# Adaptive modulations of a three-layer network: one pass before the first projection, eight passes as 1 MB steps between tiles of three projections

## The reference, cut to what matters

```python
def adaln(cv, w, b):
    m = jax.nn.silu(cv) @ w + b
    m = m.reshape(cv.shape[:-1] + (1, N_MOD, D_MODEL))
    return [m[..., k, :] for k in range(N_MOD)]
...
        a_lat = rms_norm(h_lat, g_norm_mix[i]) * (1 + sc1) + sh1
...
        h_lat = h_lat + ga1 * o_lat
        f_lat = rms_norm(h_lat, g_norm_ffn[i]) * (1 + sc2) + sh2
        h_lat = h_lat + ga2 * conv_ffn(f_lat, w_ffn_up[i], w_ffn_conv[i], b_ffn_conv[i], w_ffn_down[i])
```

## Time and profile before

| | us |
|---|---|
| median of 3 runs | 4006.7 |
| lowest, highest | 4005.63, 4010.36 |
| the profiled execution's own time | 4006.12 |
| its span, first to last instruction | 4004.3 |
| PE busy / DVE / ACT / POOL in the span | 3547.1 / 1225.7 / 778.0 / 276.0 |
| mean granted TensorE clock | 0.933 |

### The profile page before, as it was taken

One profiled execution on the slowest core, in us unless ns is written; L12 is line 12 of the kernel. 1 busy time (PEld: TensorE's weight loads), 2 busy tenths in 40 slices (PEclk: granted clock), 3 DMA queues, 4 the chain that ended last, 5 costly groups with the idle time before them and its releaser, 6 DMA issues. The chain is left out here.

```text
span 4004.3 us, 65004 instructions
## 1 busy us (share of the span) xinstructions
PE 3547.1 (89%) x26956; PEld 2168.2 (54%) x26956; DVE 1225.7 (31%) x2683; ACT 778.0 (19%) x1448; POOL 276.0 (7%) x435
## 2 busy tenths in 40 slices
PE   3699999999999999999989659996997699999984
PEld 1155755555555566444435349993573455665544
DVE  0012322222200243222017574433323433333323
ACT  0012212111100133211010243322411122222210
POOL 2000000000000000000010000000000033333320
PEclk7799999999999999999989769997998699999996
DMA  9910101111111100222221000001102289999995
GB/s 382 428 54 28 54 27 53 53 53 47 45 57 41 58 27 27 79 74 69 72 80 52 7 1 4 4 4 40 58 23 79 100 301 356 359 354 362 353 364 210
DMA packets 88964, 484.26 MB, mean 121 GB/s; under 512 B 16706, under 2 KB 20834, under 8 KB 57392
## 3 DMA queue, kind: packets, MB, share of 16 engines
q1 hardware_dynamic: 72080, 442.35, 29.7%
q0 software_dynamic: 16672, 38.77, 3.0%
HBM read 466.11 MB, written 31.46 MB: 124 GB/s over the span
## 5 line engine op out<-in xcount | busy, mean ns | idle before, releaser
L534 PE MATMUL psum<-arena 128*128 128x512 f32 x1408 | 665.3, 594 | 4.2 <-ACT arena L372 4.2
L434 PE MATMUL psum<-arena 128*128 128x512 f32 x1328 | 634.4, 601 | 34.3 <-PEq L1138 17.0
L434 PEld LDWEIGHTS psum<-arena 128*128 128x128 f32 x1328 | 254.4, 192 | 223.4 <-issue 203.9
L534 PEld LDWEIGHTS psum<-arena 128*128 128x128 f32 x1408 | 266.7, 190 | 194.4 <-issue 173.2
L2888 PE MATMUL psum<-arena 128*64 128x256 f32 x3072 | 352.7, 378 | 14.5 <-DMA arena<-exp_w_in 14.1
L2888 PEld LDWEIGHTS psum<-arena 128*64 128x64 f32 x3072 | 231.3, 134 | 161.3 <-issue 54.3
L562 DVE SCALAR_TENSOR_TENSOR arena<-psum,arena 128x511 f32<-128x511 f32 (+1 forms) x132 | 83.2, 658 | 554.1 <-ACT arena L546 554.1
L536 PEld LDWEIGHTS psum<-arena 128*128 128x128 f32 x704 | 133.4, 190 | 170.5 <-issue 170.5
L536 PE MATMUL psum<-arena 128*128 128x256 f32 x704 | 210.1, 379 | 0.0
L436 PEld LDWEIGHTS psum<-arena 128*128 128x128 f32 x640 | 121.8, 190 | 156.2 <-issue 156.2
L546 ACT ACTIVATE arena<-psum,arena 128x768 f32<-128x768 f32 (+1 forms) x88 | 77.9, 885 | 644.0 <-PE psum L536 390.2
(11 more groups left out here) (487 smaller groups left out, 4769.9 us busy)
## 6 DMA issues: line engine op xcount, KB each, us to landing
arena<-exp_w_in SPq DMA_DIRECT2D x207, 1024.0 KB, 11.2
arena<-w_mod_r_in SPq DMA_DIRECT2D x18, 4096.0 KB, 23.9
arena<-w_ffn_up_in SPq DMA_DIRECT2D x88, 512.0 KB, 3.5
arena<-w_ffn_down_in SPq DMA_DIRECT2D x16, 1408.0 KB, 5.9
arena<-w_in_in SPq DMA_DIRECT2D x35, 512.0 KB, 3.5
arena<-yrows SPq DMA_DIRECT2D x4, 4096.0 KB, 12.7
arena<-w_even_in_in SPq DMA_DIRECT2D x17, 512.0 KB, 3.6
arena<-w_qkv_in SPq DMA_DIRECT2D x12, 512.0 KB, 3.5
```

The costliest lines, as they stand in the source:

```text
L434: mm = pe.matmul(ps[:, 2 * b, :], lhsT, src[:, k, 0:LAT], start=(k == 0), stop=(k == kt - 1))
L534: mm = pe.matmul(ps[:, 2 * b, :], lhsT, A[:, k, 0:LAT], start=(k == 0), stop=(k == KD - 1))
```

## The change

`modulations` becomes `first_modulations` with pass 0 alone: eight DMAs of 1 MB (128 partitions of 8 KB out of rows of 32 KB) into eight slots, eight steps of four calls, one `turn`. X is now the first DMA on POOL's queue. The sum of squares moves from POOL to ACT (squares) and DVE (sums), behind the wait for all six DMAs. Three weight tiles of `even_in` are begun instead of five.

The other eight passes are 64 steps of a class `Mods`, each a load of 1 MB on SP and four calls on PE. `even_in` does passes 1 and 2, one step after each of tiles 0 to 15, with one slot (its feed has three slots instead of five); both `ffn_up` do three passes each, a step after each of tiles 2 to 25, with two slots. ACT's copy, PE's `turn` and DVE's additions stand one, two and three tiles after the last step of a pass; those of pass 2 stand at the end of `even_in`. PSUM banks 6 and 7 hold the passes' sums, so the projections' tiles go round three pairs of banks instead of four, and `EV_JOBS` has u and r tiles between the vt jobs.

The layout of the matrices in HBM is unchanged. The core of the diff:

```diff
-        evi = Feed(nc, "evi", io["w_even_in"], KD)
-        modulations(nc, m, io, evi)
+        evi = Feed(nc, "evi", io["w_even_in"], KD, 3)
+        first_modulations(nc, m, io, evi)
...
-        even_in(nc, m, io, evi, Norm(m, T, 0, (0, 0)), tables)
+        even_in(nc, m, io, evi, Norm(m, T, 0, (0, 0)), tables, Mods(m, io, [1, 2], [OFF["W"] + 3 * KD * P], [6, 7]))
...
-        ffn_up(nc, m, 0, T, up, Norm(m, T, 1, (0, 3)), down)
+        spare = [BIG + (KF + 4) * T + u * MOD_PASS for u in range(2)]
+        ffn_up(nc, m, 0, T, up, Norm(m, T, 1, (0, 3)), down, Mods(m, io, [3, 4, 5], spare, [6, 7]))
...
-        ffn_up(nc, m, 1, LAT, up, Norm(m, LAT, 3, (1, 3)), down)
+        ffn_up(nc, m, 1, LAT, up, Norm(m, LAT, 3, (1, 3)), down, Mods(m, io, [6, 7, 8], spare, [6, 7]))
...
+class Mods:
...
+    def load(self, e, s, i):
+        n, k = self.passes[i // KD], i % KD
+        if i >= self.R:
+            e.wait_ge(s["mdm"], i - self.R + 1)
+        e.dma_start(self.m["at"](self.slots[i % self.R], MOD_PASS),
+                    self.w[(2 * n + k // 4) * P:(2 * n + k // 4 + 1) * P, k % 4 * MOD_PASS:(k % 4 + 1) * MOD_PASS]
+                    ).then_inc(s[f"mdw{i % self.R}"], 16)
+    def step(self, pe, s, i):
+        u, k = i // KD, i % KD
+        b = self.bank(u)
+        pe.wait_ge(s[f"mdw{i % self.R}"], 16 * (i // self.R + 1))
+        if k == 0 and u >= len(self.banks):
+            pe.wait_ge(s["mde"], 2 * (u - len(self.banks) + 1))
+        silu_c = self.m["at"](OFF["silu"], 2, KD, 32)[:, self.passes[u] // (2 * MOD_PASSES), k, :]
+        w = self.m["at"](self.slots[i % self.R], 4, 512)
+        for j in range(4):
+            mm = pe.matmul(self.m["ps"][32 * j:32 * j + 32, b, :], silu_c, w[:, j, :], start=(k == 0), stop=(k == KD - 1))
+        mm.then_inc(s["mdm"], 1)
...
+    def rows(self, act, s, u):
+        act.wait_ge(s["mdm"], KD * (u + 1))
+        if u:
+            act.wait_ge(s["mdt"], u)
+        act.activation(self.rows_at, self.m["ps"][:, self.bank(u), :], ACT.Copy).then_inc(s["mdr"], 1)
...
+    def turn(self, pe, s, u):
+        pe.wait_ge(s["mdr"], u + 1)
+        for c in range(4):
+            t = pe.matmul(self.m["ps"][:, self.bank(u), 8 * c:8 * c + 8], self.rows_at[:, c * P:(c + 1) * P], self.pick,
+                          start=True, stop=True)
+        t.then_inc(s["mdt"], 1)
...
+    def between(self, e, s, first, w):
+        i = w - first + self.R - 1
+        if self.R <= i < self.N:
+            self.load(e, s, i)
+    def begin(self, e, s):
+        for i in range(min(self.R, self.N)):
+            self.load(e, s, i)
...
+def first_modulations(nc, m, io, then):
+    mods = Mods(m, io, [0], [BIG + u * MOD_PASS for u in range(KD)], [0])
...
-            for n in range(CH):
-                u = n % NS
-                if n >= NS:
-                    sp.wait_ge(s["mm"], n - NS + 1)
-                sp.dma_start(slots[:, u, :, :].rearrange("p k n -> p (k n)"),
-                             io["w_mod_r"][n * P:(n + 1) * P, :]).then_inc(s[f"w{u}"], 16)
+            mods.begin(sp, s)
...
+            pool.dma_start(X, io["xT"].rearrange("(k p) n -> p k n", p=P)).then_inc(s["x"], 16)
             for name in ("ident", "ones", "bones", "rw_masks", "rst64"):
                 pool.dma_start(m[name], io[name]).then_inc(s["x"], 16)
-            pool.dma_start(m["X"], io["xT"].rearrange("(k p) n -> p k n", p=P)).then_inc(s["x"], 16)
...
-            ss, sq, X = m["at"](NRM_SS, T), m["at"](NRM_SQ, 2, T), m["X"]
-            pool.tensor_tensor(ss, X[:, 0, :], X[:, 0, :], MUL).then_inc(s["ss"], 1)
-            for k in range(1, KD):
-                if k >= 3:
-                    pool.wait_ge(s["ss"], k - 1)
-                pool.tensor_tensor(sq[:, k % 2, :], X[:, k, :], X[:, k, :], MUL).then_inc(s["sq"], 1)
-                pool.wait_ge(s["sq"], k)
-                pool.wait_ge(s["ss"], k)
-                pool.tensor_tensor(ss, ss, sq[:, k % 2, :], ADD).then_inc(s["ss"], 1)
...
-            for n in range(NP):
...
+            act.wait_ge(s["x"], 16 * 6)
+            for k in range(KD):
+                if k >= 3:
+                    act.wait_ge(s["ss"], k - 2)
+                act.activation(ss if k == 0 else sq[:, k % 2, :], X[:, k, :], ACT.Square).then_inc(s["sq"], 1)
+            mods.rows(act, s, 0)
...
+            for i in range(KD):
+                mods.step(pe, s, i)
+            pe.wait_ge(s["x"], 16 * 6)
+            mods.turn(pe, s, 0)
...
+            for k in range(1, KD):
+                dve.wait_ge(s["sq"], k + 1)
+                if k >= 2:
+                    dve.wait_ge(s["ss"], k - 1)
+                dve.tensor_tensor(ss, ss, sq[:, k % 2, :], ADD).then_inc(s["ss"], 1)
...
+    def __init__(self, nc, name, w, kt, slots=None):
         self.w, self.kt, self.n = w, kt, w.shape[0]
-        self.slots = 2 * KF // kt
+        self.slots = slots or 2 * KF // kt
...
+        for w in range(1, self.n):
+            t = w + self.slots - 1
+            if t < self.n or between is not None:
+                e.wait_ge(mm, w)
+            if t < self.n:
+                self.load(m, e, t)
+            if between is not None:
+                between(w)
...
-            feed.rest(m, sp, s["mm"])
+            mods.begin(sp, s)
+            feed.rest(m, sp, s["mm"], lambda w: mods.between(sp, s, 2, w))
...
-                b = t % 4
+                b = t % 3
                 feed.arrived(pe, t)
-                if t >= 4:
-                    pe.wait_ge(s["tp"], t - 3)
-                if t == 3:
+                if t >= 3:
+                    pe.wait_ge(s["tp"], t - 2)
+                if t == 2:
                     pe.wait_ge(s["nxn"], KD)
...
                 mm.then_inc(s["mm"], 1)
+                u, k = (t - 2) // KD, (t - 2) % KD
+                if 0 <= t - 2 < mods.N:
+                    mods.step(pe, s, t - 2)
+                if u and k == 1 and u <= len(mods.passes):
+                    mods.turn(pe, s, u - 1)
...
+                u, k = (t - 2) // KD, (t - 2) % KD
+                if u and k == 0 and u <= len(mods.passes):
+                    mods.rows(act, s, u - 1)
...
+                u, k = (t - 2) // KD, (t - 2) % KD
+                if u and k == 2 and u <= len(mods.passes):
+                    mods.add(dve, s, u - 1)
...
 EV_JOBS = [("z", 0), ("q", 0), ("q", 1), ("k", 0), ("k", 1), ("v", 0), ("g", 0), ("v", 1), ("g", 1), ("v", 2), ("g", 2), ("v", 3),
-           ("g", 3), ("u", 0), ("vt", 0), ("u", 1), ("vt", 1), ("u", 2), ("vt", 2), ("u", 3), ("vt", 3),
-           ("r", 0), ("r", 1), ("r", 2), ("r", 3)]
+           ("g", 3), ("u", 0), ("u", 1), ("vt", 0), ("u", 2), ("vt", 1), ("u", 3), ("vt", 2), ("r", 0), ("vt", 3),
+           ("r", 1), ("r", 2), ("r", 3)]
...
-    wg = at(OFF["W"] + feed.slots * KD * P, 2, 256)
+    wg = at(EV_WG, 2, 256)
...
-            feed.rest(m, sp, s["mm"])
+            mods.begin(sp, s)
+            feed.rest(m, sp, s["mm"], lambda w: mods.between(sp, s, 0, w))
...
-                sp.wait_ge(s["mm"], feed.last_over(lo, lo + n))
+                if lo < feed.slots * KD * P:
+                    sp.wait_ge(s["mm"], feed.last_over(lo, lo + n))
                 if lo + n > feed.slots * KD * P:
+                    sp.wait_ge(s["mdm"], mods.N)
+                if lo + n > EV_WG - OFF["W"]:
                     sp.wait_ge(s["gp"], 4)
...
-                b = j % 4
-                if j >= 4:
-                    pe.wait_ge(s[released[EV_JOBS[j - 4]][0]], released[EV_JOBS[j - 4]][1])
+                b = j % 3
+                if j >= 3:
+                    pe.wait_ge(s[released[EV_JOBS[j - 3]][0]], released[EV_JOBS[j - 3]][1])
...
+                if t == 0:
+                    pe.wait_ge(s["nxn"], KD)
+                if t < mods.N:
+                    mods.step(pe, s, t)
+                if t == KD + 1:
+                    mods.turn(pe, s, 0)
+            mods.turn(pe, s, 1)
...
+                if tiles[kind, i] in (KD, 2 * KD):
+                    mods.rows(act, s, tiles[kind, i] // KD - 1)
...
+            mods.add(dve, s, 0)
...
+            mods.add(dve, s, 1)
```

More of the change, by code:

```diff
@@ L175, with __init__, bank, add @@
 MOD_PASSES = MT * P // MOD_PASS
[L178 to L190 removed]
+class Mods:
+    def __init__(self, m, io, passes, slots, banks):
+        self.m, self.passes, self.slots, self.banks = m, passes, slots, banks
+        self.w = io["w_mod_r"]
+        self.R, self.N = len(slots), KD * len(passes)
+        self.SEMS = " mdm mdr mdt mde mdg " + " ".join(f"mdw{u}" for u in range(self.R)) + " "
+        self.rows_at = m["at"](OFF["rows"], 512)
+        self.pick = m["ident"].rearrange("p (j c) -> p j c", j=4)[:, :, 0:2]
+    def bank(self, u):
+        return self.banks[u % len(self.banks)]
+    def load(self, e, s, i):
[27 more added lines that the diff above has]
+        t.then_inc(s["mdt"], 1)
+    def add(self, dve, s, u):
+        m, n = self.m, self.passes[u]
+        l, t = n // MOD_PASSES, n % MOD_PASSES
```

(34 more changed lines are left out.)

76 lines of the change are left out of this document (12 added, 64 removed).

## The result

| | before | after |
|---|---|---|
| median, us | 4007.73 (4 runs) | 3919.85 (4 runs) |
| lowest, highest | 4005.63, 4010.36 | 3918.07, 3922.76 |
| span of the profiled execution | 4004.3 | 3916.3 |
| mean granted TensorE clock | 0.933 | 0.946 |

The ratio is 0.9781, with an interval of 0.9764 to 0.9798: 88 us faster, where 70 were forecast. Nine later runs of before and five of the changed kernel gave 4007.16 and 3922.19, ratio 0.9786 (0.9773 to 0.9799).

What follows compares the result with a forecast made beforehand. The first stage was taken as bound by its DMA loads, the projections by PE. From 4006.1 us, 158 saved in front and 88 added by steps and turns gave 3936, range 3914 to 3966.

Steps and rivals of the forecast that it cites:

- rival 5: Cheap seams and a fast front: 0.95 us a step, X at 36, time 3915; chance 0.07.
- When X is there: Front: X with the tables arrives at 38 us, between 36 and 41, reckoned from the bytes and queue rates.
- rival 2: Front: X comes as late as before, the front ends at 64, time 3951; chance 0.08.
- Squares and sums: Front, after X: two squares on ACT, then seven sums on DVE with handing over, 9.1 us in all.
- The tail: Front, after the sums: bank copy and `turn` run beside the last sum; DVE's bias and gains add 0.5 us.
- A step: Projections: four calls cost 1.25 us, 0.86 of it streaming and 0.39 array-shape changes; 64 steps are 80 us.
- Turn: Projections: `turn` after a pass's last step adds 1.0 us of weight loads; seven stand between tiles, 7 us.
- Its end in `even_in`: The eighth `turn`, of pass 2, with its copy and additions at the end of `even_in`: 0.8 us.
- What was put at nothing: Projections: loads, SP's waits, three pairs of banks, ACT's copies and DVE's additions are all covered, costing nothing.
- The 1 us of lost clock at `even_in`'s start: Norm's first PE calls run at half clock from the start, behind a front that is mostly waiting: 1 us more.
- signs named ahead: Marks of being right: `even_in`'s start, DMA share in front, gapless PE, tile distances, clock of 1.00, longer stage spans.
- Rivals 1 to 4: Dear seams, 3964, chance 0.10; late X, 3951, 0.08; slow strided loads, 3960, 0.05; steps lowering the clock, 4042, 0.04.

Runs made afterwards that it cites:

- e1: Changed kernel without passes 1 to 8 (no loads, steps, turns or additions; modulations zero, so routing differs): 3862.8 us.
- e4: Kernel before with only three pairs of PSUM banks instead of four and the changed order of jobs: 4012.06 us against 4007.49 of before beside it.
- e9: The changed kernel, unaltered, timed again as yardstick over five runs: median 3922.19 us, ratio to before 0.9786.
- e7: Changed kernel with the matrices laid out so that each 1 MB load is contiguous instead of 8 KB rows 32 KB apart: 3917.19 us.

## Why the prediction came out as it did

The direction, the bound and the mechanism were right, and the range held the time. 3919.85 lies 16 us under the 3936, outside the forecast's own 3924 to 3950 and nearer to rival 5 (cheap seams and a fast front, 3915). By terms, in the profile's ledger:

- **When X is there: the step that failed.** Bytes were counted as if X were through only when everything was ("the bytes take 38.4 us"), and 38 was taken. The row says 31.15. Both queues had work all the time, but POOL's short list got 0.377 of the engines and was through while SP's still had 2.7 of its 10.4 MB to go. The finish of a short list depends on its queue's share, not on the sum of bytes. But the only share that the trace of before holds, 0.213, would have given some 50 us (4.13 MB at 0.213 of 401 GB/s, and 2 us), which is rival 2: the 0.377 beside rows of 8 KB could not be read from it. 6.9 us too much.
- The Trainium skill's page "DMA: Bandwidth & Descriptors", section "SWDGE vs HWDGE vs iDMA", says that an engine goes round its internal queues in turn, and that the two kinds of issuer feed different ones. The trace agrees that neither waits for the other; its shares of 0.377 and 0.635 are with rows of 3 KB and 8 KB, those of 0.213 and 0.768 before with 3 KB and 32 KB.
- **Squares and sums** from 31.15 to 40.1 are 9.0 us, forecast 9.1. **The tail** behind them was put at 0.5 and took 1.9: `turn` ran at half rate, and began at 39.48 because ACT's copy stood behind the eighth square. The barrier was 0.87 (0.8). Together the front came out 5.6 us earlier than forecast.
- **A step**: 1.25 forecast, 1.20 measured. The 0.39 from a job g is 0.34. The estimate from the Trainium skill's page "TensorE: Matmul & The Clock Gate", section "Single matmul latency", gave 1.19 by way of 0.166 us at either seam, a constant that the page states for a single bf16 matmul. The runs agree with the sum, twice 0.17; in the rows the two sides are 0.20 and 0.14.
- **Not every seam was new.** In `even_in` eight steps stand beside a job g or vt, where the array changed its shape before as well. Timeline of ACT in the changed kernel, two tiles with a job g between them:

```profile
121.76 0.81 ACT L862 ACTIVATE arena<-psum 128x768 f32<-128x768 f32 x1 [10.73 <-PE psum L822]
...
134.78 0.81 ACT L862 ACTIVATE arena<-psum 128x768 f32<-128x768 f32 x1 [9.64 <-PE psum L822]
```

  13.02 against 12.03: 1.0 a step, not 1.2. Eight at 1.2, eight at 1.0, a turn of 0.9 and 0.66 at the end are 19.2, and e1 gives 19.1. The prediction's 16 x 1.25 missed this though the table of jobs showed it.
- **Turn**: 1.0 forecast, 0.9 measured. Its end in `even_in`: 0.8 forecast, 0.66.
- **What was put at nothing** was nothing: the loads (PE waits for none of them in the projections), SP's waits, three pairs of banks (e4), ACT's and DVE's parts. The 1 us of lost clock at `even_in`'s start came as forecast (1.1), but e4 had it too, with the long front: the number was right by luck as much as by its reason.
- **Left over.** Front 5.6 and steps 6.2 us explain 11.8 of the 18.0 between forecast and ledger. Of the other 6, 2.4 are in both `ffn_up`, beyond what e1 shows the steps to cost, and 3.2 in the rest. e9's profile repeats the code without 4 of them, net: 1.7 go with the clock of `ffn_up` 0 and 2.9 with the two levels of the rest, as shown above, and smaller differences run both ways. Yet e9's median is 85 us under before, where the terms as measured (164.4 - 1.1 - 81.8) give 81.5. Of these 3.5, 1.0 is that before's profiled execution was under its median; the others lie in small pieces, the largest 0.7 and 0.6 in the two `ffn_down`, and no run says why. Whether the kernel before, whose profile and e4's both had the slower level in the rest, can take the faster one too, and what picks it, stays open.

Of the signs named ahead, DMA above 0.9 in front, the tile distance (save the 1.0 beside a job g or vt), the gapless PE and the clock of 1.00 came as said. `even_in`'s start (46 to 52) and the stage spans (23 and 33 longer) did not; they carry the sizes above. Rivals 1 to 4 fell: a step at 1.20 and not 1.69, X at 31 and not 54, e7 for the stride, and no clock under 1.00 between tiles.

## What to carry to other kernels

Loads that bound a stage can go under a stage that PE bounds, but the PE work goes with them at its full price: here a stage bound by its loads got 164 us shorter, and 82 us of work came in elsewhere. Put such foreign groups of matmuls next to places where the array changes its shape anyway, or next to each other, since each separate place costs a fixed 0.34 us. And when a DMA-bound stage shrinks, look at what it covered: 9 us of squares came into the open here, 25 if they had stayed on POOL, and squaring as the pieces land won back 5.2 of the 9.
